# Five modulation slots in a two-block transformer kernel move: four out of the second layer's mixer into the norm ahead of its projection, one into the second block's first norm

## The reference, cut to what matters

```python
def ada_chunks(cvec, w, b):
    m = jax.nn.silu(cvec) @ w + b
    return jnp.split(m[..., None, :], 6, axis=-1)

def modulate(x, g, shift, scale):
    return rms_norm_2(x, g) * (1 + scale) + shift
...
        hn = rms_norm(h, norm_mix_g[l])
        proj = hn @ w_in[l]
...
        h = h + jnp.concatenate([o_attn, o_rec], axis=-1) @ w_out[l]
```

## Time and profile before

| what | us |
|---|---|
| median of 3 runs | 1693.22 |
| lowest and highest | 1692.78, 1693.87 |
| the profiled execution, whole | 1691.35 |
| its span in the profile | 1689.6 |

### The profile page before, as it was taken

How to read it: one execution, slowest core, us unless ns; L and a number is a source line. 1 busy time by engine, 2 the same in 40 slices (tenths; PEclk the granted TensorE clock), 3 DMA queues, 4 the chain that set the end, 5 groups by cost and what they waited for, 6 DMA issues and landing times.

```text
span 1689.6 us, 28191 instructions
## 1 busy us (share of the span) xinstructions
PE 1616.5 (96%) x11870; PEld 1407.3 (83%) x11870; DVE 1017.9 (60%) x1577; ACT 870.0 (51%) x1467; POOL 21.1 (1%) x38
## 2 busy tenths in 40 slices
PE   6999999999999999999989999999999898999997
PEld 6968999989789999987648777888888674789997
DVE  7675545465856555724555764424555777687585
ACT  6764534448545344544564543323444547766563
POOL 0000000000000000300000000000000000000000
PEclk9999999999999999999999999999999999999998
DMA  7465445354556464772202452232213530164642
GB/s 298 145 245 210 160 157 202 135 191 143 200 187 240 152 233 145 220 222 75 75 1 73 177 200 101 86 125 100 84 53 125 200 125 26 52 224 154 233 146 92
DMA packets 60524, 253.94 MB, mean 150 GB/s; under 512 B 4976, under 2 KB 8304, under 8 KB 42480
## 3 DMA queue, kind: packets, MB, share of 16 engines
q1 hardware_dynamic: 59088, 249.01, 41.6%
q0 software_dynamic: 1312, 3.15, 1.0%
HBM read 251.09 MB, written 1.05 MB: 149 GB/s over the span
## 4 chain that ended last, share of the span: by engine, by line
PE 81%; DVE 10%; ACT 6%; issue 2%; DMA 0%; SPq 0%; DVEq 0%; ACTq 0%
PE PA L917 63%; PE PA L977 3%; DVE W_t L1572 2%; PE PB L1340 2%; PE PB L852 2%; PE PA L1005 2%; ACT W_t L2299 1%; PE PB L1327 1%; PE PA L954 1%; PE PA L959 1%; PE PA L953 1%; PE PA L872 1%; PE PB L1270 1%; ACT tmp L2742 1%; PE PA L1412 1%
## 5 line engine op out<-in xcount | busy, mean ns | idle before, releaser
L917 PE MATMUL PA<-XH_t,W_t 128*128 128x256 f32 (+2 forms) x3968 | 873.3, 314 | 4.1 <-DVE W_t L1572 1.8
L917 PEld LDWEIGHTS PA<-XH_t,W_t 128*128 128x128 f32 x3968 | 650.1, 188 | 59.8 <-issue 6.0
L1572 DVE TENSOR_TENSOR W_t<-raw,W_t 128x1024 fp32r<-128x1024 f32 (+1 forms) x344 | 445.0, 1298 | 306.1 <-ACT W_t L2299 305.7
L917 PE MATMUL PA<-XL_t,W_t 128*128 128x256 f32 (+2 forms) x1984 | 620.5, 313 | 0.0
L2299 ACT ACTIVATE W_t<-raw 128x1024 fp32r<-128x1024 f32 (+1 forms) x344 | 381.4, 1113 | 155.6 <-PE PA L917 136.5
L917 PEld LDWEIGHTS PA<-XL_t,W_t 128*128 128x128 f32 x1984 | 373.1, 188 | 23.2 <-issue 0.5
L917 PE MATMUL PA<-AH_t,W_t 128*128 128x256 f32 (+2 forms) x1232 | 266.1, 311 | 0.2
L917 PEld LDWEIGHTS PA<-AH_t,W_t 128*128 128x128 f32 x1232 | 201.2, 188 | 14.1 <-DVE AL_t L1618 0.8
L917 PE MATMUL PA<-AL_t,W_t 128*128 128x256 f32 (+2 forms) x616 | 190.7, 310 | 0.0
L2457 ACT ACTIVATE tmp<-PA,par 128x512 f32<-128x512 f32 (+1 forms) x88 | 58.4, 667 | 133.0 <-PE PA L917 125.3
L1695 DVE SCALAR_TENSOR_TENSOR tmp<-PA,par,tmp 128x510 f32<-128x510 f32 (+1 forms) x88 | 53.6, 613 | 120.5 <-ACT tmp L2457 119.6
(11 more groups left out here) (275 smaller groups left out, 1576.4 us busy)
## 6 DMA issues: line engine op xcount, KB each, us to landing
raw<-in_w_ada SPq DMA_DIRECT2D x48, 1024.0 KB, 5.1
raw<-in_w_gu SPq DMA_DIRECT2D x44, 1024.0 KB, 4.8
raw<-in_w_dn SPq DMA_DIRECT2D x64, 704.0 KB, 4.0
raw<-in_w_up SPq DMA_DIRECT2D x44, 1024.0 KB, 4.8
raw<-in_w_in SPq DMA_DIRECT2D x30, 1024.0 KB, 5.5
raw<-in_w_out SPq DMA_DIRECT2D x12, 1024.0 KB, 4.8
raw<-in_w_qkv SPq DMA_DIRECT2D x6, 1024.0 KB, 6.3
raw<-in_w_outc SPq DMA_DIRECT2D x4, 1024.0 KB, 4.8
```

The lines of the kernel that those rows point to most:

```text
L917: mm = pe.matmul(PA[:, (L.b0 + o) % 4, 0:T], W[:, c:c + P], X[:, k, L.x0:L.x0 + T], start=(n == 0 and m == 0 and not L.early), stop=(n == ...
L1572: dve.tensor_tensor(WL_t[:, w:w + L.cols], RAWV[:, r % RAW, part * UNIT:part * UNIT + L.cols], WHf[:, w:w + L.cols], ALU.subtract).then_in ...
```

## The change

Four slots of the second layer's group A (units u = 4 to 7) go to the norm ahead of its input projection: one at `start`, one `amid`, two at `end`. The seven dummies of that norm go. Their transposes (`turn`) go behind the projection's first four tiles, and the ones of the block that A now holds stay in the mixer at u = 3. In the second block's first norm a slot that stood inline, ahead of the projection's seventh tile, goes `amid`, and two of the three dummies there go; the slots of the norm and the one left inline are numbered anew. The numbering of the slots and the ring of `raw` follow. The wait ahead of the gates' weights is written so that it still names the same norm, and PE's wait ahead of the second layer's gates asks for the copied columns.

```diff
-                self.amid = 2 if lead else 0
+                self.amid = 2 if lead or held == 4 else 0
...
-            n = norm(writers, "pre", l, T1, H1, [(0, T1, ("mixg", l), None)])
+            n = mixed_in = norm(writers, "pre", l, T1, H1, [(0, T1, ("mixg", l), None)])
...
                 a = linear("copy", w_in1[l], n, T1, XV, rdy, dst=prj1, tile0=tile0,
-                           parts=None if l or tile0 else [(0, T1, rdy)])
+                           held=4 if l and not tile0 else 0, parts=None if l or tile0 else [(0, T1, rdy)])
+                if a.held:
+                    mixed_in.fill(a.slots(), start=1, amid=1, end=2)
...
                 plan.append(("linear", a))
+                if a.held:
+                    plan.append(("turn", l))
...
-            held = AdaSlots(8)
+            held = AdaSlots(4 if l else 8)
...
-                w = linear("copy", w_in2, 4, T2, XV, None, dst=prj2, held=2, ada=2,
+                w = linear("copy", w_in2, 4, T2, XV, None, dst=prj2, held=3, ada=1,
...
-                n.fill(w.slots(), start=1, end=1)
+                n.fill(w.slots(), start=1, amid=1, end=1)
...
-                            sp.wait_ge(S("n_sum"), plan[idx - 3][1].index + 1)
+                            sp.wait_ge(S("n_sum"), [x for kind, x in plan[:idx] if kind == "norm"][-1].index + 1)
...
                 if n is second_start:
-                    keep_busy(PB[:, 3, :], 3)
-                elif n.index in (2, 3):
-
-                    keep_busy(PB[:, 1, :], (2, 4)[n.index - 2])
+                    keep_busy(PB[:, 3, :], 1)
+                elif n.index == 3:
+
+                    keep_busy(PB[:, 1, :], 4)
...
                 mm.then_inc(S("n_bc"), 1)
-                if n.index == 2:
-                    keep_busy(PB[:, 1, :], 5)
...
                     if l:
 
-                        pe.wait_ge(S("ada_row"), 3)
+                        pe.wait_ge(S("ada_free"), 4)
...
-                    if u in (0, 1, 4, 5, 6, 7):
+                    if u in ((0, 1) if l else (0, 1, 4, 5, 6, 7)):
...
-                    if u in (2, 8):
+                    if u in ((2,) if l else (2, 8)):
```

## The result

The changed kernel takes 1700.75 us, the median of four executions (1699.32 to 1705.11), the kernel before 1693.0 (1692.76 to 1693.87). The ratio is 1.0045 with a 95% interval of 1.003 to 1.006: slower, by 7.75 us. The prediction was 1692.7 with a range of 1689.2 to 1696.4.

The account below looks back on a forecast made before the run. PE was busy 1616.5 of 1689.6 us, so gains lay only where it stands still; +0.15 - 1.86 - 0.3 + 1.7 - 0.2 = -0.5 us gave 1690.85 profiled, 1692.7 as median, range 1689.2 to 1696.4.

Parts of the forecast that it names:

- The fourth slot's load: End of norm index 2: lands at 367.7 us, in time for the limit of 367.9; price 0, bounds 0 to +0.5.
- the late load: Rival, norm index 2: the fourth slot's load shares engines with two others, landing at 371.5; +3.1 us, 1696.3; chance 0.13.
- the five dummies: End of norm index 2: two slots need 2.0 us where dummies took 2.3; costs nothing if their loads have landed.
- The inline slot's load: Second block's first projection: now issued second, lands at 726.0 where PE wants it at 725.38; +0.6 us, 0 to +2.
- The root and the slots at the start and amid: Norm index 2: the start slot delays the root by +0.15 us (0 to 0.3); the slot amid costs nothing.
- The gates' weights and the transposes behind the projection: Behind norm index 2: later weights cost 0 (bounds 0 to +0.5); 0.3 us of added PE transposes also cost 0.
- The slot at the end of the second norm: Second block's first norm: its load is 0.7 us late, mostly hidden by PE's wait for DVE; +0.2.
- The mixer: Second layer's mixer: scores 1.86 us earlier without the slot at u = 4, transposes -0.3, a second clock fall +1.7.
- the second fall: Second layer's mixer: emptied of slots, the clock falls again between 468 and 473 us; +1.7 us (0 to +2.6).
- The slot gone from the projection: Second block's first projection: one slot fewer inline where PE is dense; -1.0 us.

Follow-up runs that it names:

- e3: e1 with three dummies ahead of the third slot of norm index 2 and six ahead of the fourth: +1.4 us against the kernel before, ratio 1.0004.
- e1: The changed kernel with the second block's norm and projection as in the kernel before, so only the four slots move: +3.0 us against the kernel before, ratio 1.0014.
- e5: e2 with the slot left inline one place later, ahead of the projection's seventh and eighth tile: +0.4 us against the kernel before, ratio 0.9996.
- e6: e2 with POOL's 32 small loads held back until six tiles of the projection are copied: -0.1 us against the kernel before, ratio 0.9999.
- e4: e1 without the two slots at the end of norm index 2 and their loads, five dummies back: -1.4 us against the kernel before, ratio 0.9985.
- e7: e1 with the fourth slot ahead of the projection's third tile and three dummies ahead of the third slot: +1.1 us against the kernel before, ratio 1.0002.
- e2: The kernel before with only the second block's norm changed (third held slot, one left inline): +5.2 us against the kernel before, ratio 1.003.
- the second part mended: The change to the second block's first norm and projection, with POOL's small loads started later; alone it is e6, -0.1 us against the kernel before.
- e9: e7 plus two dummies each at u = 5, 6, 7 of the second mixer, e2's change and POOL's later loads: -2.1 us against the kernel before, ratio 0.9991.

## Why the prediction was wrong

**The fourth slot's load (0, bounds 0 to +0.5) is the first step that failed.** The mechanism and its limit were right: issue right behind the first slot (predicted 1.1 us after it, measured 363.41 - 362.28 = 1.13), and a landing later than 367.9 costs every microsecond. The landing was wrong. In the time of before the load landed at 370.5 - 1.27 = 369.2, not 367.7, and the 1.3 to 1.6 us past the limit are the 1.7 that e3 measured. It took 7.1 us (in e1 and e3 7.4). From 366.5 to 370.4 us, between the third slot's landing and its own, the queue moved 1.60 MB, more than its one megabyte, so it shared with the chunk issued behind it at 364.65 too. I had such a sharing as the rival "the late load", with 371.5, and gave it 0.13. I also put +0.5 as the upper bound of the step while my own upper landing, 368.4, stood beside a limit of 367.9, so the bound held no error of the load's time at all.

**The clock in the norm is missing from the sum: +2.5 us (e1 less e3).** I priced the five dummies at the PE time they freed and never as cover. I had reckoned with the clock only in the mixer, though I wrote that the fourth slot might wait 1 to 2 us with nothing ahead of it. The wait itself became 3.02 us.

**The inline slot's load (+0.6, bounds 0 to +2) failed worst.** I said that "both orders move the same two megabytes, so I take 726.0". The load landed at 736.1 - 5.66 = 730.5 in the time of before; PE waited 5.06 us, and with the clock it made +6.4. It failed because the order does matter beside POOL's queue: the slot's load behind a chunk came 9.4 us after it, where the chunk behind a slot had come 5.0 after it, and in e5 a slot took 9.5 and a chunk 4.7. Without POOL's loads (e6) PE doesn't wait at all. Why the one suffers more is the open point above. POOL's loads were in the trace of before at the same microseconds, and I had not looked at what was being moved there. What I left out was another queue.

**What held.** The root and the slots at the start and amid: 0.15 predicted, 0 in e4. The gates' weights and the transposes behind the projection: 0, and the ACT copies at 381 and 440 us of before stand 5.38 and 5.41 us later. The slot at the end of the second norm: 0.50 of wait and +0.1 behind it (predicted +0.2). The mixer: -1.86 - 0.3 + 1.7 = -0.46 predicted, with the second fall as forecast: it begins at 475.4 us, which is 470 in the time of before (I had said 468 to 473), and ends in the early output tiles; the median of e4 says -1.4, e1's less the norm's 4.2 says -1.2, and e3's and e7's less their norms say -0.3 and -0.1. The size is right within what can be told. The slot gone from the projection: -1.0 predicted, -1.2 and -0.8 in e6 and e5.

**The sum by what was measured.** Norm +4.2 for +0.15, mixer about -0.8 (the mean of the last four) for -0.46, projection and its norm +3.9 (e2's profile) to +6.5 (the changed kernel's) for -0.2: together +7.3 to +9.9, and 7.75 was measured. The error lies in two loads and in the clock behind them; the mixer's -0.8 is a difference of medians and profiles and no better than 1 us.

**The range** was built from the bounds of the terms, and both failing terms had bounds that took the load's time as known. A range that let each load be late by what one more megabyte costs (my own 3.2 us of the rival), and the clock fall behind each wait, would have reached about 1700, by my estimate: 1692.7, 3.2 twice, and some of the clock.

## What to carry to other kernels

A slot that fills a norm needs its load there, and the load needs its buffer: write for each moved load who frees the buffer, when, what it then shares engines with, and let every one of these be late in the range. Where a change takes dummies away and leaves work that waits for a load, count the clock behind that wait too; dummies ahead of a late load don't bring it sooner but won 2.5 us here. Before moving work out of a crowded place, look whether only one of its pieces is on the path: moving that one a few steps in both mixers, with the second part mended, gave -3.8 us, and moving four away was part of +7.8.

## What the runs showed of the hardware

The spread of one kernel goes with its clock. Beside the experiments the kernel before ran 92 times, in three sets, from 1688.79 to 1697.46 us: at a mean clock of 0.994 to 0.996 mostly 1690 to 1693, at 0.990 always 1695.8 or more. A stretch of 3.4 us at 0.50 costs about 1.5 (the one at 161 us shifted everything by 1.51), and such stretches come and go in the same code: at about 161 us in three of the fourteen profiles, between 1322 and 1336 us in eight, and in the first mixer in all but one (e5), for 3.4 us or for 6.8. The first four executions of the kernel before lay within 1.1 us of each other and hid that. Between sets of three or four, 0.2% was too fine a claim.

A megabyte in 2 KB pieces took 3.9 us behind another load with no second queue running, and 9.5 beside POOL's loads; one in 8 KB rows took 2.5 and 4.7. While the slot came beside POOL's loads, both queues moved the same 0.70 MB in 6 us.

An idle of 1.5 to 2.3 us that no semaphore ended stood in the mixer's first slots in the profiles of the changed kernel, e7 and e9, three of fourteen. What it is stays open.
